# A four-layer hybrid encoder on eight cores: one transpose per tile for the rotary and key-value latents, the A heads' gates moved by one head, and other places for four kinds of loads

## The reference, cut to what matters

```python
for l in range(DEPTH):                       # 4
    shift, scale, gate = split(silu(c) @ w_mod[l] + b_mod[l], 3)
    h = rmsnorm(x, g_pre[l]) * (1 + scale) + shift
    y = mla_band_mixer(h, ...) if l % 2 == 0 else spatial_gating_mixer(h, ...)
    x = x + gate * rmsnorm(y, g_post[l])

def mla_band_mixer(h, ...):
    cq, ckv, kr, bq, bk, bv, gate = split(h @ w_in, [512, 256, 64, 1024, 1024, 1024, 2048])
    q = rmsnorm(cq, g_q) @ w_uq              # 8 heads of 128 + 64, the 64 rotated by position
    kv = rmsnorm(ckv, g_kv) @ w_ukv          # 8 heads of 128 (k) + 128 (v)
    k = concat(kv[..., :128], rope(kr))      # the rotated 64 are shared by the heads
    oa = chunk_causal_attention(q, k, kv[..., 128:])         # "A" heads 0 to 7
    ob = chunk_band_attention(bq, bk, bv, rel_table)         # "B" heads 8 to 15, 9 chunks of 64
    return (concat(oa, ob) * silu(gate)) @ w_out

def spatial_gating_mixer(h, ...):
    u, v, gate = split(h @ w_in, 3)          # 2048 each
    sv = (per group of 128 positions: masked w_s @ layernorm(v)) + b_s
    return (u * sv * silu(gate)) @ w_out
```

## Time and profile before

| | us |
|---|---|
| median of 3 executions (4821.66 to 5615.1) | 4829.51 |
| the profiled execution | 4851.75 |
| its span on the slowest core (core 1), the one that the rows show | 4850.2 |
| spans of the eight cores | 4810.9 to 4850.2 |
| PE busy on core 1 | 4318.7 (89%) |
| DVE, ACT, POOL busy | 1793.9, 1188.8, 461.6 |

### The profile page before, as it was taken

How to read it: one execution, slowest core, us unless ns; L and a number is a source line. 1 busy time by engine, 2 the same in 40 slices (tenths; PEclk the granted TensorE clock), 3 DMA queues, 4 the chain that set the end, 5 groups by cost and what they waited for, 6 DMA issues and landing times.

```text
span 4850.2 us, 80970 instructions; the slowest of 8 cores (4810.9 to 4850.2 us)
## 1 busy us (share of the span) xinstructions
PE 4318.7 (89%) x30884; PEld 2446.2 (50%) x30884; DVE 1793.9 (37%) x3721; ACT 1188.8 (25%) x2187; POOL 461.6 (10%) x514
## 2 busy tenths in 40 slices
PE   0367889999999899999999788899999999999999
PEld 0135666666644344444444566666665444444444
DVE  0643332333346426211365333333334742611023
ACT  1113443222233213100222244322222321300011
POOL 1020010000000001222002100000000000122200
PEclk9989999999999999999999899999999999999999
DMA  9965664552396878456857455453429675732543
GB/s 195 189 100 90 102 103 58 70 65 31 42 205 194 167 160 207 81 83 93 202 187 115 70 84 81 61 62 58 47 35 187 194 170 132 176 35 35 78 162 134
DMA packets 632075, 550.92 MB, mean 114 GB/s; under 512 B 417376, under 2 KB 563040, under 8 KB 607632
## 3 DMA queue, kind: packets, MB, share of 16 engines
q0 software_dynamic: 321760, 239.09, 36.5%
q1 hardware_dynamic: 309936, 306.65, 22.4%
HBM read 620.54 MB, written 100.76 MB: 149 GB/s over the span
## 4 chain that ended last, share of the span: by engine, by line
PE 78%; DMA 9%; DVE 4%; issue 3%; SPq 3%; another core or an unknown queue 2%; ACT 1%; POOL 0%; DVEq 0%; ACTq 0%; POOLq 0%
PE PS L300 74%; PE PS L298 4%; SPq L337 3%; DMA W<-ab_w_in 2%; DVE RG L319 1%; DMA RG<-sg_w_out 1%; DMA VR<-R 1%; ACT R L310 1%; DMA RG<-w_mod 1%; DMA RG<-R 1%; DMA R<-MODROW 1%; DVE R L325 1%; DMA R<-VR 1%; DMA RG<-W 0%
## 5 line engine op out<-in xcount | busy, mean ns | idle before, releaser
L300 PE MATMUL PS<-W,RG 128*128 128x128 bf16 (+3 forms) x13696 | 1527.5, 264 | 188.5 <-DVE RG L319 66.9
L300 PE MATMUL PS<-RG,W 128*128 128x512 bf16 x6464 | 1492.5, 381 | 70.0 <-DVE RG L319 63.7
L310 ACT ACTIVATE R<-PS 128x512 bf16<-128x512 f32 (+5 forms) x1536 | 780.3, 515 | 2589.8 <-PE PS L300 1654.4
L300 PEld LDWEIGHTS PS<-W,RG 128*128 128x128 bf16 x13696 | 1051.3, 99 | 702.5 <-issue 232.1
L300 PE MATMUL PS<-RG 128*128 128x512 bf16 (+2 forms) x4480 | 1077.3, 377 | 26.6 <-DMA RG<-sg_w_out 15.7
L300 PEld LDWEIGHTS PS<-RG,W 128*128 128x128 bf16 x6464 | 628.0, 98 | 789.6 <-issue 110.0
L300 PEld LDWEIGHTS PS<-RG 128*128 128x128 bf16 x4480 | 440.3, 98 | 480.9 <-issue 40.5
L300 PE MATMUL PS<-R 128*128 128x512 bf16 (+3 forms) x1604 | 396.9, 297 | 26.1 <-ACT R L310 13.4
L310 ACT ACTIVATE RG<-PS 128x2048 bf16<-128x2048 f32 (+2 forms) x128 | 151.6, 1184 | 881.6 <-PE PS L300 863.4
L322 DVE TENSOR_TENSOR RG<-PS,R 128x512 bf16<-128x512 f32 x128 | 88.5, 692 | 712.4 <-PE PS L300 710.6
L325 DVE CAST R<-PS 128x512 bf16<-128x512 f32 (+1 forms) x352 | 234.4, 667 | 231.4 <-PE PS L300 188.3
(11 more groups left out here) (81 smaller groups left out, 1831.2 us busy)
## 6 DMA issues: line engine op xcount, KB each, us to landing
W<-w_mod POOLq DMA_DIRECT2D x64, 1024.0 KB, 9.5
RG<-w_mod POOLq DMA_DIRECT2D x32, 1024.0 KB, 18.9
W<-ab_w_in POOLq DMA_DIRECT2D x64, 512.0 KB, 8.7
VR<-R SPq DMA_DIRECT2D x128, 256.0 KB, 3.4
R<-VR SPq DMA_DIRECT2D x32, 1024.0 KB, 6.3
W<-sg_w_in POOLq DMA_DIRECT2D x32, 1024.0 KB, 15.5
XB<-R SPq DMA_DIRECT2D x20, 1024.0 KB, 8.8
R<-XB SPq DMA_DIRECT2D x20, 1024.0 KB, 6.3
```

The lines of the kernel that those rows point to most:

```text
L300: P.op("pe", lambda e: e.matmul(o, lhsT, rhs, start=start, stop=stop), r=r, w=w, sig=sig)
L310: P.op("act", lambda e: e.activation(out=o, in_=i, func=func, **kw), r=r, w=w, wp=wp)
```

## The change

Five things change; no arithmetic does, and the number of matmuls, activations and transfers stays the same.

1. **Low-rank pass.** Each tile has its own staging pieces, `stage(a, t)` of one piece (8 tiles in turn), and is transposed at once: one transpose of 128x512 into four chunks for `ckv` (chunks 8 to 11) and one for `qr` (chunks 4 to 7). The chunks of the rotary queries, of the key-value latent and of the gates change to fit (`ROPE_C`, `YC`).
2. **Gates.** Head n's gate is computed in the fill of head n itself, with q, k, v of head n + 1; ahead of the heads only q, k, v of head 0 remain (`fill_pre`). The groups stand in another order, with `pause` items between that emit nothing but count in the pacing. `fin` makes sure that its gate is there. `poll` does nothing while a gate waits in `later`. Gate weights have a load of their own, `ldg`.
3. **Value weights of B heads.** `ldv` is issued from the fill: behind the last gate of head 7, then behind the last `vb_fill` that reads the old ones. `vb_fill(0)` goes to the end of its list.
4. **Odd layers.** The third column group of w_out is loaded in pass 9 into `R`, and the boundary goes through the groups in the order 3, 2, 0, 1; the places of `x` that this takes are made up for in `G[hx]`, in eight pieces of 1 KB per partition (`b3`). The setup of layer 1 and 3 is cut in three, the first pass's mod steps stand later (0.6 and 0.75 of it), and `v_load` is issued one step earlier.
5. `load_wout`, the even boundaries and the startup stay as they were.

```diff
-                a += 4 * (t // 4 % 2)
-                return Rb(a, 4).rearrange("p (c t d) -> p c t d", t=4, d=128), RT(a, 4)
+                a += t % 8
+                return Rb(a, 1), RT(a, 1)
...
+                dmaT(Y[:, 8:12, tile(t)], sv, r=svt, w=gt(yr, range(8, 12), [t]))
...
-                tt("pool", sv[:, :, q, :], m1.rearrange("p (c d) -> p c d", d=128), m2.rearrange("p (c d) -> p c d", d=128), ALU.add,
-                   r=m1t + m2t, wp=svt)
+                tt("pool", sv, m1, m2, ALU.add, r=m1t + m2t, w=svt)
+                dmaT(Y[:, 4:8, tile(t)], sv, r=svt, w=gt(yr, range(4, 8), [t]))
...
             def fill_a(n):
+                g = [gate_fill(n, tg) for tg in range(4)]
+                if n == 7:
+                    return g[0] + g[1] + g[2] + g[3] + pause(3) + [(lambda: ldv(0), 0.0), (lambda: (twos(8), twos(9)), 0.0)] + fill_b(8)
+                q = [qk_fill(n + 1, "q", tg) for tg in range(4)]
+                k = [qk_fill(n + 1, "k", tg) for tg in range(4)]
+                v = [va_fill(n + 1, tg) for tg in range(4)]
+                p1, p3 = pause(1), pause(3)
+                return (g[0] + g[1] + p3 + q[0] + q[1] + p1 + k[0] + p1 + k[1] + p1 + g[2] + p3 + v[0] + p1 + v[1] + p1 + q[2] + p1 + q[3] + p1
+                        + g[3] + p3 + k[2] + p1 + k[3] + p1 + v[2] + p1 + v[3])
...
                     for t2 in range(4, 8):
                         fs += vb_fill(m // 2, t2)
+                    if m < 7:
+                        fs.append((lambda: ldv(m // 2 + 1), 0.0))
...
-                if fb["busy"] is not None:
+                if fb["busy"] is not None or later:
                     return
...
+            if hx is None:
+                return b3(Rf(24 + 8 * k, 8)), RT(24 + 8 * k, 8)
+            return G[hx][:, 8 * k:8 * k + 8, 1024:1536].bitcast(F32), gt(hx, range(8 * k, 8 * k + 8), range(8, 12))
...
+                        if p == 9 and s == 7:
+                            wload(Rb(24, 16).rearrange("p (k c) -> p k c", c=512), sg_w_out[i, :, 1024:1536], RT(24, 16))
...
-                                if tg < 3:
+                                if tg < 2:
```

More of the change, by code:

```diff
@@ L430, in h_scale, with boundary @@
             c, s_ = newst()
-            act(ht, x, AF.Square, r=xt, w=s_ + htt, accum=st[:, c:c + 1])
+            act(b3(ht), x, AF.Square, r=xt, w=s_ + htt, accum=st[:, c:c + 1])
             rs = rstd_of(c, s_, D)
-            stt("dve", x, x, rs, Rf(A_KB, 8), ALU.mult, ALU.mult, r=xt + s_ + RT(A_KB, 8), w=xt)
+            stt("dve", x, x, rs, b3(Rf(A_KB, 8)), ALU.mult, ALU.mult, r=xt + s_ + RT(A_KB, 8), w=xt)
         def h_shift(x, xt, ht, htt, hr, t):
-            tt("dve", ht, x, Rf(B_KB, 8), ALU.add, r=xt + RT(B_KB, 8), w=htt)
+            tt("dve", b3(ht), x, b3(Rf(B_KB, 8)), ALU.add, r=xt + RT(B_KB, 8), w=htt)
             dmaT(G[hr][:, :, tile(t)], ht, r=htt, w=gt(hr, T16, [t]))
-        def boundary(l, yr, wout, corder, Xcur, Xnext, last, begun=None):
+        def boundary(l, yr, ym, wout, corder, Xcur, Xnext, last, begun=None, odd=False):
+            hx = 1 - yr if odd else None
             def loadx(t):
-                x, xt = xbuf(t)
-                dma("sp", x, Xcur[tile(t), :], r=[X_t[id(Xcur)][t]], w=xt)
+                x, xt = xbuf(t, hx)
+                dma("sp", x, b3(Xcur[tile(t), :]), r=[X_t[id(Xcur)][t]], w=xt)
             def chain_a(t):
@@ L452, in chain_a @@
                 stt("dve", ps, ps, rs, Rf(0, 8), ALU.mult, ALU.mult, r=s_ + RT(0, 8), w=pt)
[L453 to L454 removed]
+                tt("dve", x, x, b3(ps), ALU.add, r=pt + xt, w=xt)
+                dma("sp", b3(Xnext[tile(t), :]), x, r=xt, w=[X_t[id(Xnext)][t]])
             def chain_b(t):
[L457 removed]
+                x, xt = xbuf(t, hx)
                 ht, htt = htbuf(t)
@@ L526, in stage @@
             def stage(a, t):
-                a += 4 * (t // 4 % 2)
-                return Rb(a, 4).rearrange("p (c t d) -> p c t d", t=4, d=128), RT(a, 4)
-            for k in range(2):
-                sv, svt = stage(8, 4 * k)
-                mset("dve", sv[:, 2, :, 64:128], 0.0, w=svt)
-                mset("dve", sv[:, 3, :, 0:64], 0.0, wp=svt)
+                a += t % 8
+                return Rb(a, 1), RT(a, 1)
+            for t in range(8):
+                sv, svt = stage(8, t)
+                mset("dve", sv[:, 320:448], 0.0, w=svt)
             def swap(v):
@@ L625, in even_layer @@
             gk = {"k": 0}
+            gate_done = set()
             later = []
@@ L711, in done @@
                     act(th, bank(b), AF.Tanh, r=[PS_t[b]], w=tht, scale=0.5)
-                    later.append([6, b, lambda: stt("dve", Y[:, n, tgs(tg)], th, 1.0, bank(b), ALU.add, ALU.mult, r=[PS_t[b]] + tht,
-                                                    w=gt(yr, [n], range(4 * tg, 4 * tg + 4)))])
+                    later.append([6, b, lambda: stt("dve", Y[:, yc[n], tgs(tg)], th, 1.0, bank(b), ALU.add, ALU.mult, r=[PS_t[b]] + tht,
+                                                    w=gt(yr, [yc[n]], range(4 * tg, 4 * tg + 4))), (n, tg)])
+                    gate_done.add((n, tg))
                 return group(items, done)
@@ L827, in fill_b @@
                         fs.append((lambda tg=tg: load_wout(tg), 0.0))
+                if m == 0:
+                    for tg in range(4):
+                        fs += vb_fill(0, tg)
                 return fs
@@ L952, in fin @@
             def fin(n, g, pr):
+                while (n, g) not in gate_done:
+                    fstep()
+                if any(e[3] == (n, g) for e in later):
+                    flush(lambda e: e[3] == (n, g))
                 b = obank(n, g, pr)
@@ L993, in even_layer, with fstep @@
             twos(1)
-            for f, c in fill_a(0):
+            fq = {"fl": fill_pre(), "em": 0.0, "n": 0, "hj": 0}
+            def fstep():
+                f, c = fq["fl"].pop(0)
                 f()
+                fq["em"] += c
                 tick()
-            flush(lambda e: True)
+                poll(fq["n"], fq["hj"])
+            while fq["fl"]:
+                fstep()
             LA = 4
-            fl = []
-            tot = em = 0.0
-            hj = 0
+            tot = 0.0
             cur[0] = -1
@@ L1086, in setup, with setup2 @@
                 mset("dve", on, 1.0, w=ont)
-            def setup2(bsr, bsrt, on, ont):
-                for half in range(2):
+            def setup2(bsr, bsrt, on, ont, half):
+                if True:
                     b = nb()
@@ L1378, in wo @@
                     def wo(cg, n):
-                        if cg < 3:
+                        if cg < 2:
                             return G[hr][:, n, cg * 512:(cg + 1) * 512], gt(hr, [n], range(4 * cg, 4 * cg + 4))
+                        if cg == 2:
+                            return Rb(24 + n, 1), RT(24 + n, 1)
                         return Wb(n, 1), WT(n, 1)
-                    boundary(l, yr, wo, (3, 0, 1, 2), Xcur, Xnext, last)
+                    boundary(l, yr, range(16), wo, (3, 2, 0, 1), Xcur, Xnext, last, odd=True)
                     if not last:
```

157 lines of the change are left out of this document (64 added, 93 removed).

## The result

The change makes the kernel faster by 2.3%: over the executions in which both dies ran at the same granted clock, here and in all times below, the median is 4713.9 us against 4824.8, and the ratio is 0.977, with a 95% interval of 0.975 to 0.979. A second chip gave 0.974 (0.972 to 0.977). The forecast of 4660 us had the sign and two thirds of the size: 111 us were gained by the medians (138 by the two profiled executions, 4851.75 and 4713.94) where 168 were forecast. The result lies in the stated range of 4600 to 4740, but above the forecast's own range of 4620 to 4700.

A forecast was written before the change was run, and what follows sets the result against it. PE, busy 89% of the span, was taken as the bound, its waits as the gain: 64 + 57 + 25 + 22 = 168 us, 4851.75 to 4684, less 22.2 to the median, 4660 us; range 4600 to 4740.

The forecast's parts named there:

- Values' weights: Heads 7 to 15: loads issued early in the head before remove PE's whole waits, 56.8 us (45 if one load stays late).
- Gates: Heads 0 to 6: gate waits of 105.6 us fall to 35, copies cost 6; gain 64 us (30 to 95).
- For each gate I count in the new order what PE has to do between its end and the next use of its bank: Heads 0 to 6: 7.2, 2.5, 1.4 and 1.7 us against 2.7 needed; waits of 0, 0.2, 1.3, 1.0 us.
- Rival 1: Heads 0 to 6: pauses too short, each gate still waits 1.5 us, gain only 22 us; 4702 us, chance 0.15.
- Low-rank pass and head 0: Up to and including head 0: 19 + 16 - 4 + 22 - 28 = 25 us gained, head 0's gates returning in the heads.
- link: Low-rank pass: each rotary add waits for the previous tile's transpose; add 1.2, landing 2.4, passing on 0.3: 4.0 us, 14 a layer.
- 4 us off for the mod loads that POOL issues at that moment: End of the low-rank pass: mod loads beside the last transposes reduce the gain by 4 us.
- Rival 2: Low-rank pass: serial chain at crowded landings of 8.0 or 11.3 us loses 157 or 249 us; chances 0.07 and 0.05.
- Rival 3: Low-rank pass: strided transposes each land 1.0 us later, 28 us lost; 4688 us, chance 0.07.
- The 45 us of the forecast's bracket: Low-rank pass and head 0: upper gain, 45 us, if each link takes 3.6 us.
- Odd layers: Layers 1 and 3: earlier loads of w_out and v weights remove waits, 15.7 - 4 + 2 + 8 = 22 us (0 to 30).
- Rival 4: Early loads of w_out and v weights push others into PE's way; 39 us come back, 4699 us, chance 0.08.

The follow-up runs named there:

- the run with the old place: Changed kernel with values' weight loads for the second to fourth pair of heads issued again at the start of heads 9, 11 and 13: 4767.7 us, ratio 0.986.
- the earlier place alone: Changed kernel with a gate's multiply put into DVE's queue three fill steps after the gate's end instead of six, pauses kept: 4662.3 us, ratio 0.964.
- loads held: Changed kernel with the two mod loads at the end of the low-rank pass held until the last tile's transposes have landed: 4690.1 us, ratio 0.970.
- pieces spread: Changed kernel with staging pieces used in the order 0, 2, 4, 6, 1, 3, 5, 7: 4683.5 us, ratio 0.969.
- a fifth edit: Third group of w_out loaded in pass 6 instead of 9, not run alone; with the four other edits on the changed kernel: 4594.5 us, ratio 0.951.

## Why the prediction was right, and where it was off

**Values' weights** (57 forecast, 69.6 measured on core 1, 60.5 on cores 2 to 7): right in mechanism, and the run with the old place shows for three of the four pairs that the issue point alone does it. That the size is close on cores 2 to 7 is in part luck. The forecast counted the 28.9 us of layer 2, which are those of core 1; cores 2 to 7 of the same execution waited 15.4 to 17.1 us there, core 3 for instance:

```profile
PE PS L300 <- DMA W<-ab_w_in: 17.0, 4, 5.4
```

And it counted the waits only. Behind a wait PE works on at a lower granted clock. The same stretch from head 8 to head 9, with the wait of the earlier trace rows, before and then after (window, length, busy us and instructions of PE, PEld, DVE, ACT and POOL, granted clock, share of DMA, GB/s):

```profile
912.70:959.10 46.40, 36.84 (x311) 23.04 (x309) 13.95 (x39) 7.71 (x17) 5.37 (x5) 0.89 0.74 87
```

```profile
887.20:922.60 35.40, 35.00 (x311) 22.34 (x309) 14.65 (x39) 7.70 (x17) 4.13 (x4) 1.00 0.67 72
```

The same 311 instructions of PE are busy for 36.84 us at a granted clock of 0.89, a mean over its two levels of 2.4 and 1.2 GHz in a stretch in which PE stood for 9.16 us, and for 35.00 us at 1.00. So 1.8 us come on top of the wait.

**Gates** (64 forecast, 39.3 measured): the failed step is "For each gate I count in the new order what PE has to do between its end and the next use of its bank". The count was set against 2.7 us from the gate's end to the release, as if that were a duration. It is the place of the `stt` in DVE's queue, which the code sets by steps of the fill, and which both traces show behind a memset and a copy. Rival 1 gives nearly the size that was measured (1.1 us a gate where it had 1.5) for a reason that the runs refute: with the pauses as they are and the earlier place alone, 27.0 of 31.1 us went. One of the signs of being wrong, more than 10 us of waits for copies in a layer, is met in layer 0 when heads 7 to 15 are counted with the others (9.6 and 3.2 us).

**Low-rank pass and head 0** (25 forecast, 3.4 measured, 27.5 less 24.1 for head 7; 9.2 on cores 2 to 7): link, landing and head 0's own work came out as worked out (3.83 us against 4.0; 2.3 against 2.4; 10.3 us from PE's first matmul of the fill at 368.12 to head 0's first score at 378.47 against 11; head 7 12 us longer against 14). The failed term is "4 us off for the mod loads that POOL issues at that moment". The last transposes would have landed at 353.1 by their issue and 2.3 us, and the forecast had 353.5; DVE saw them at 367.20. The loads cost 14 us a layer there, and 24 us came back when they were held. The trace of before had the price: in 340 to 375 of it, beside the same mod loads, the landings were

```profile
W<-w_mod POOLq DMA_DIRECT2D x2, 1024.0 KB, 13.5
RG<-R SPq DMA_TRANSPOSE x10, 14.7
```

The 8.0 of the earlier trace rows mixed these with earlier ones, and the forecast set it aside by the number in flight, not by what else was in flight. Rival 2's serial chain was real (30 us when undone) but at the uncrowded price. Rival 3 did not happen: 2.3 us with four separate chunks as target. The rule behind it (the Trainium skill, "DMA: Bandwidth & Descriptors", section "Latency and other measured facts") is not borne out for this shape. As an estimate from that section's figures, 400 against 261 GB/s, a landing of 2.4 us would be up to 1.3 us longer, where the forecast said at most 1. The 45 us of the forecast's bracket don't follow either: a link shorter by 0.4 us makes 28 x 0.4 = 11 us, and the sum 36.

**Odd layers** (22 forecast, 28.4 measured on core 1, 15.2 on cores 2 to 7): the waits for `sg_w_out` went, as did that of 6.4 us. But the 5.3 us for `sg_w_out` in layer 3 stood on core 1 alone, and cores 2 to 7 gained nothing from the end of layer 2's heads on (1131.7 to 1135.3 us before, 1131.8 to 1138.5 after). The 2 us given to layer 1's first pass were not there (13.9 us of one wait in place of 8.5, 4.3 and 1.0), and the 4 us taken back appeared for `sg_w_in`, not for `w_mod`. Rival 4's collisions happened mainly where it did not look, at the end of the low-rank pass. **Strided x** cost nothing: an output tile of layer 1 takes 13.8 us as before, as from 2334.11 to 2347.93:

```profile
2334.11 3.62 PE L300 MATMUL PS<-W,RG 128*128 128x512 bf16 x16
...
2347.93 3.62 PE L300 MATMUL PS<-W,RG 128*128 128x512 bf16 x16
```

**From the profiled execution to the median**: 22 us were taken off because the median of before stood so far under its profiled execution. The changed kernel's profiled execution lies on its median (both 4713.9), so the 22 us belong to that execution of before (on the fourth chip two others, of 4860 and 4866 us, are as slow). With the terms' net error (about 30 us by the profiled executions) this makes the 54 us between 4660 and 4714. The trace of before shows where core 1 lost them: its span is 29 us above the median of cores 2 to 7 (4850.2 and 4821.1), with 10 of them in heads 8 to 15 of layer 2 and 16 from there to the end. Those are stretches whose waits parts 3 and 4 had already counted as gains, so a part of the same time was taken off twice; how much, one profiled execution can't tell. Why cores 0 and 1 were slow there stays open.

## What to carry to other kernels

A time "from the end of A to the release of its bank" is only a duration if the releasing instruction was already in its engine's queue; look at what stands in front of it there, since moving an issue point by three steps was worth 52 us, and the pauses, which make room on PE, were worth next to nothing without that. Price a small transfer by what else is in flight in the same few microseconds, in a window as narrow as the event: it took 2.3 us without large loads and 16 beside 2.5 MB of them, and loads with a late user can be held for it. Read a wait on several cores before counting it as a gain: the 28.9 us of the slowest core were some 16 on six others. Where one wait in a stretch is removed, ask for the next one behind it before counting the gain: in layer 1's first pass the transpose, the weights and the mod load took turns until the order of the loads was changed.

## What the runs showed that was not expected

- A 128x512 transpose from SP lands in 2.3 us (the median of 33 in one pass), and reaches its user 16.4 us (layer 0) and 13.7 us (layer 2, 2617.40 to 2631.11) after its issue when POOL issues two loads of 1 MB and one of 0.5 MB within 2 us of it.
- A wait of some 9 us on PE cost 1.6 to 1.8 us more in the work behind it, with a granted clock of 0.89 (912.7 to 959.1) and 0.92 (1057.6 to 1102.8) in such stretches of before, and of 1.00 in the same ones after; 39.8 us of waits put back cost 52 us on the same core.
- Gains added up, even of two edits in the same stretch (loads held and pieces spread): 24, 30, 52 and 3 us one by one, 116 together with a fifth edit.
